# State-space scan of a hybrid decoder on one Trainium2 core: turned sample states as the moving operand in four column groups, decay products of two heads in alternation

## The chip, the cores and the metric

One core of a Trainium2 chip (TRN2) runs the whole program. The metric is the device time of one execution in microseconds, lower is better. Time before: 2363.76 us, the median of 3 runs (2363.07 to 2365.89).

## The reference, cut to what matters

The program is one inference step of a two-layer decoder trunk for a prompt of 256 tokens and 8 samples of 4 new tokens each. Layer 0 is a mixer of gated linear attention and mLSTM, layer 1 a Mamba-2 state-space mixer of 64 heads in 8 groups, with a head size of 64 and a state of 128. The change is in the scan of layer 1:

```
cb = jnp.einsum('bign,bjgn->bijg', cc, bc)
y_intra = jnp.einsum('bijgh,bjghp->bighp', cb[..., None] * decay, dtc[..., None] * xc)
y_inter = jnp.einsum('bign,bghpn->bighp', cc, s) * jnp.exp(acum)[..., None]
s_new = jnp.exp(a_last)[..., None, None] * s + jnp.einsum('bjgh,bjghp,bjgn->bghpn', w, xc, bc)
```

For a sample, `s` is the state that it brings (64 heads x 64 x 128), `cc` its C rows (4 tokens), and `y_inter` is what the old state adds to the output of the new tokens.

## The kernel before, in words

Activations lie turned, with channels on partitions and 288 columns: 256 of the prompt and 32 of the samples (sample b has columns 256 + 4b to 256 + 4b + 3). Weights are float32 and are split on the chip into a high and a low part: ScalarE casts a unit of 128x4x256 (line 126), VectorE subtracts (line 132), and TensorE makes 24 products of 288 columns with it (`project_unit`, lines 145 to 147). Four units are one quad of 256 output columns. TensorE raises the semaphore `used` at the end of a unit; ScalarE may then cast four units further on into the same buffer, and VectorE's split follows that cast.

`ssd_mixer` goes through the 8 groups of layer 1 in rounds (`turns`). A round projects group gg (5 quads, 20 units) and does the scan of the group before, G, in 20 steps between the units: step k stands behind unit k on TensorE, ScalarE and VectorE. There are eight groups, so there is a first round with projections alone, seven with both, and a last one with the scan of group 7 alone. `T_STEPS` (line 1805) is the order of TensorE's jobs, written by hand: steps 0 and 1 turn x and form C by B, step 2 turns B and the first sample's state (`st0`, line 1739), steps 2 to 9 turn the eight states and multiply them with C (`in0` to `in7`, `t_inter`, lines 1742 to 1751), steps 5, 6, 10 and 11 make the state updates (`u0` to `u7`, line 1760), steps 12 to 15 make the output of the prompt and the samples (`t_y`, lines 1773 to 1785), two heads at a time, called a quarter here, and step 18 makes the sums for the norm.

The jobs of `RING` go round three PSUM banks; those of `OWN`, `inter` among them, use a fourth. A bank is taken with a wait on the semaphore `free` and is given with `full`.

`t_inter` for sample b takes the turned state (128x512 in `stT`, two buffers by turns, written by ScalarE at line 1885) as four stationary operands of 128x128, each with the four columns of C of that sample as moving operand, all through the helper at line 1699. ScalarE may overwrite a buffer when `st_used` says so. In step 11 VectorE, behind its updates of the states (`v_update`, line 2026), multiplies the result by the exponentials of the samples (line 2079) into `inter`, and in steps 12 to 15 it adds `inter` to the output (`v_y`, line 2038).

`t_y` makes for each of two heads three products, also through line 1699: x by decay with 256 moving columns, the same with 128, and the samples' own with 32 rows and 32 columns. The first head writes partitions 0 to 63 of the bank, the second 64 to 127.

Layer 0 has helpers that matter for comparison: line 775 multiplies the samples' states with a wide query in four column groups, line 784 makes the output of a head, the last product of which sums over samples with `fold` (128x32), and line 712 makes blocks of 64 columns on two column groups.

VectorE's work for the next group (`v_prep`, lines 1942 to 1995) has the causal convolution in steps 12 to 15 and the preparation of the stacked operands in step 17. `cth` holds the tanh of the convolution between ScalarE's step 16 and VectorE's step 17. `gates1` (line 1422) makes the decay columns for the whole layer before the scan: it writes nine 64x128 blocks into `pad`, TensorE turns them, and VectorE copies them into `cols`.

Of the kernel before, what the change touches and what calls it, by code (L numbers as in the profile page):

```python
# [1411 lines left out]

K_C0, K_C1, K_CS, K_C01, K_D0, K_D1, K_DS, K_W0, K_W1, K_N = range(10)


def layer1_buffers(core, ctx):
# [3 lines left out]
def gates1(nc, core, io, scr, g):  # L1422


    with ExitStack() as tmp:
# [49 lines left out]
        @block.vector  # L1475
        def _(dve):
            st = Steps(dve, dve_s)
            dve.memset(pad[:], 0.0)
            st.then_wait(dve.tensor_copy(keep2[:], core.keep[0:64]))
            dve.memset(keep2[:, P:P + 1], 0.0)  # L1480
            dve.wait_ge(s_in, 32)
            dve.tensor_scalar(dt[:], core.bank[0][0:64, 0:T], par[:, 0:1], None, ALU.add).then_inc(u_d, 1)
            dve.wait_ge(sp_d, 1)

            st.then_wait(dve.scalar_tensor_tensor(dt[:], dt[:], 0.0, au[:], ALU.max, ALU.add))
            st.then_wait(dve.tensor_scalar(c[:], dt[:], par[:, 1:2], None, ALU.mult))
            st.then_wait(dve.tensor_tensor_scan(c[:], keep2[:], c[:], 0.0, ALU.mult, ALU.add))
            cs = samples(c[:, S0:T])
            dve.tensor_scalar(negc[:], c[:], -1.0, None, ALU.mult).then_inc(nc_d, 1)
            dve.tensor_scalar(we[:, TS:2 * TS], c[:, S0:T], -1.0, None, ALU.mult)  # L1490
            st.then_wait(dve.tensor_tensor(tot[:], c[:, P - 1:P], c[:, TP - 1:TP], ALU.add))
            dve.tensor_scalar(wx[:, 0:P], c[:, 0:P], tot[:], None, ALU.subtract)
            dve.tensor_scalar(wx[:, P:TP], c[:, P:TP], c[:, TP - 1:TP], None, ALU.subtract)
            dve.tensor_tensor(samples(wx[:, S0:T]), cs, cs[:, :, TD - 1:TD].broadcast_to([64, NB, TD]), ALU.subtract
                              ).then_inc(wx_d, 1)
            dve.tensor_copy(pad[:, 0:TP], c[:, 0:TP])
            dve.tensor_copy(pad[:, K_CS * P + 96:K_CS * P + P], c[:, S0:T])
            dve.tensor_scalar(pad[:, K_C01 * P:K_C01 * P + P], c[:, 0:P], c[:, P - 1:P], None, ALU.subtract)
            dve.tensor_copy(pad[:, K_D0 * P:K_D0 * P + TP], dt[:, 0:TP])
            dve.tensor_copy(pad[:, K_DS * P + 96:K_DS * P + P], dt[:, S0:T])  # L1500
            dve.wait_ge(wx_e, 1)
            dve.tensor_tensor(pad[:, K_W0 * P:K_W0 * P + TP], wx[:, 0:TP], dt[:, 0:TP], ALU.mult)
            dve.tensor_tensor(we[:, 0:TS], wx[:, S0:T], dt[:, S0:T], ALU.mult).then_inc(pad_d, 1)
            dve.wait_ge(turned, 1)
            for i in range(3):
                dve.tensor_copy(g["hist"][:, 16 * i:16 * i + 16].rearrange("p t c -> p (t c)"), core.bank[5 + i][:, 0:384])
            dve.wait_ge(turned, 2)
            dve.tensor_copy(g["cols"][:, 0:8].rearrange("p n h -> p (n h)"), core.bank[1][:, :])
            st.then_wait(dve.tensor_copy(g["cols"][:, 8], core.bank[2][:, 0:64]))


def ssd_mixer(nc, core, io, out, scr, g, ws):
# [6 lines left out]
    with ExitStack() as tmp:  # L1519
# [16 lines left out]
        stT, state = sb("state_turned", [P, 2, 512]), sb("state", [P, NB, 4, SSD_N])  # L1536
        y = sb("y", [P, 4, T])
        inter = sb("inter", [P, 4, TS])
        var, r, t1 = (sb(n, [P, T]) for n in ("var", "r", "t1"))
        pst = sb("prompt_state", [P, 4, P])  # L1540
        tail = sb("tail", [P, 6, 27])
# [197 lines left out]
                i = pe.transpose(bk[:, q * P:(q + 1) * P], state[:, b, q], core.ident[:])  # L1739
            i.then_inc(full_, 1)  # L1740

        def t_inter(pe, b, G):

            bk, full_ = fill("inter")
            if b == 0:
                wait_free(pe, "inter", G)
            wait_read(pe, f"st{b}", G)
            for q in range(4):
                i = mm(pe, bk[:, q * TS + TD * b:q * TS + TD * b + TD], stT[:, b % 2, q * P:(q + 1) * P],
                       xbc[:, 5, S0 + TD * b:S0 + TD * b + TD], start=True, stop=True)  # L1750
            i.then_inc(s["st_used"] if b < NB - 1 else full_, 1)

        def t_update(pe, i, G):

# [18 lines left out]
        def t_y(pe, q, G):  # L1773
            bk, full_ = fill(f"y{q}")
            wait_free(pe, f"y{q}", G)
            pe.wait_ge(s["decays"], G * 4 + (q + 1))
            if q == 0:
                pe.wait_ge(s["xsd"], G + 1)
            for hh in range(2):
                h = 2 * q + hh  # L1780
                o, c = slice(64 * hh, 64 * hh + 64), slice(64 * h, 64 * h + 64)
                mm(pe, bk[o, 0:256], xdt[:, 0, c], PP[:, h, 0:256], start=True, stop=False)
                mm(pe, bk[o, 128:256], xdt[:, 1, c], PP[:, h, 256:384], start=False, stop=True)
                i = mm(pe, bk[o, S0:T], xsr[96:128, c], PP[96:128, h, 384:416], start=True, stop=True)
            i.then_inc(full_, 1)

        def t_tail(pe, part, gg):
# [8 lines left out]
        def t_rms(pe, G):  # L1796
# [3 lines left out]
            for q in range(4):  # L1800
# [1 line left out]
            i.then_inc(full_, 1)  # L1802


        T_STEPS = {0: ("x0", "x1"), 1: ("stack", "cb"), 2: ("brow", "st0"), 3: ("st1", "in0", "st2"),
                   4: ("in1", "st3", "in2"), 5: ("u0", "u1", "in3"), 6: ("u2", "u3"), 7: ("st4", "st5"), 8: ("st6", "in4", "in5"),
                   9: ("st7", "in6"), 10: ("u4", "u5", "in7"), 11: ("u6", "u7"), 12: ("y0",), 13: ("pstate", "y1"),
                   14: ("y2",), 15: ("y3",), 18: ("rms",)}

        def t_step(pe, k, G):  # L1810
# [60 lines left out]
        def a_step(act, k, G, st):  # L1871
# [6 lines left out]
                act.activation(brow[:].rearrange("p j n -> p (j n)"), bk[:, 0:256], ACT.Copy).then_inc(s["brow"], 1)  # L1878
            for b in {2: (0,), 3: (1, 2), 4: (3,), 7: (4, 5), 8: (6,), 9: (7,)}.get(k, ()):
                bk = wait_full(act, f"st{b}", G)  # L1880
                if b >= 2:
                    act.wait_ge(s["st_used"], G * 7 + (b - 1))
                else:
                    act.wait_ge(s["tail_out"], (G + 1) * 96)
                act.activation(stT[:, b % 2], bk[:, :], ACT.Copy).then_inc(free[at(f"st{b}", 0)[0]], 1)
            if k in (5, 6):
                for q in ((0, 1), (2, 3))[k - 5]:
                    act.wait_ge(s["args"], G * 4 + (q + 1))
# [53 lines left out]
        def v_prep(dve, k, gg, st):  # L1942
# [30 lines left out]
            if k == 17:  # L1973
# [12 lines left out]
                hi = stack[:].bitcast(F32R)  # L1986
                dve.tensor_copy(hi[:, :, 0:TS], inter[:])
                dve.tensor_copy(hi[:, :, TS:2 * TS], inter[:])
                b_ = xbc[:, 4, S0:T]
                bh = bstack[:].bitcast(F32R)  # L1990
                dve.tensor_copy(bh[:, 0:TS], b_)
# [39 lines left out]
        def v_y(dve, q, G, st):  # L2031
# [3 lines left out]
            dve.scalar_tensor_tensor(y[:, q], xbc[:, q], dd[:, q:q + 1], bk[:, 0:T], ALU.mult, ALU.add  # L2035
                                     ).then_inc(free[at(f"y{q}", 0)[0]], 1)
            wait_read(dve, f"y{q}", G)
            st.then_wait(dve.tensor_tensor(y[:, q, S0:T], y[:, q, S0:T], inter[:, q], ALU.add))
            dve.tensor_tensor(y[:, q], y[:, q], zt[:, q], ALU.mult).then_inc(s["gated"], 1)

        def v_step(dve, k, G, st):
# [34 lines left out]
                dve.sem_inc(s["zg"], 1)  # L2076
            if k == 11:
                bk = wait_full(dve, "inter", G)
                dve.tensor_tensor(inter[:], bk[:, 0:4 * TS].rearrange("p (q t) -> p q t", q=4),
                                  we[:, :, TS:2 * TS], ALU.mult).then_inc(free[0], 1)  # L2080
                wait_read(dve, "inter", G)
                dve.sem_inc(s["we_used"], 1)
            if 12 <= k <= 15:
# [15 lines left out]
        def _(dve):  # L2099
            st = Steps(dve, s["dve"])  # L2100
            dve.memset(cbm[0:96, 384:416], 0.0)
            dve.memset(PP[0:96, :, 384:416], 0.0)
            st.then_wait(dve.memset(xp[:, :, 0:3], 0.0))
            dve.sem_inc(s["conv_in_used"], 1)
# [74 lines left out]
```

## Time and profile before

| | |
|---|---|
| median of 3 runs | 2363.76 us |
| the runs | 2363.07 to 2365.89 us |
| the profiled execution | 2366.03 us, its span 2364.6 us |
| mean granted clock of TensorE | 0.956 |
| TensorE busy, matmul | 2195.0 us, 93% |
| TensorE busy, weight loads | 2054.8 us, 87% |
| VectorE busy | 1438.9 us, 61% |
| ScalarE busy | 938.1 us, 40% |
| GpSimd busy | 279.1 us, 12% |
| state products of layer 1 | 66.7 us, 512 records |

How to read it: an fp32 product that is no transposition has two records in the trace, since it goes through the array in two passes; a split one (float32r) has one. Matmuls are pipelined, and their records overlap: what a product costs the queue is the distance from its start to the start of the next one, not its duration. The line of a product that was made by the helper `mm` is that of the helper, 1699, so those are told apart by their tiles and shapes. Times in the timeline are from the start of the span.

### The profile page before, as it was taken

The page shows a single profiled execution, that of the slowest core. Times are in us where ns is not written, and L with a number is a line of the kernel's source. Part 1 is how long each engine was busy: PE and PEld are TensorE (multiplying, and loading weights), DVE is VectorE, ACT ScalarE, POOL GpSimd, SP SyncE. Part 2 cuts the span into 40 slices and gives each one's busy share as a digit, 9 for nine tenths or more (in the row PEclk, how much of TensorE's full clock was granted, in tenths as well). Part 3 has the DMA queues.
Part 4 walks back from the last instruction along what each step waited for, and adds up shares of the span by engine and source line. Part 5 has one row for each costly group of instructions (what it writes and reads, how often), then busy time and mean ns, then how long its engine had stood idle before and what let it go on. Part 6 is the DMA issues. An engine that isn't in the chain of part 4 may idle for free. (4 is left out here: it accounts for less than half of the span.)

```text
span 2364.6 us, 42336 instructions
## 1 busy us (share of the span) xinstructions
PE 2195.0 (93%) x15490; PEld 2054.8 (87%) x15490; DVE 1438.9 (61%) x2784; ACT 938.1 (40%) x1260; POOL 279.1 (12%) x423
## 2 busy tenths in 40 slices
PE   6699999999999999959997899999999999859997
PEld 4698989999998998829997899989999999749996
DVE  5553756648475665744335377778778877844333
ACT  3444443444343343323333344544544435323332
POOL 1100201112001020210000102122121121210000
PEclk8799999999999999979998899999999999869999
DMA  3664858667657584747443656656565565336442
GB/s 103 215 176 127 278 157 271 195 223 239 188 172 252 151 278 121 241 168 241 153 160 120 194 144 187 181 180 189 169 189 181 159 195 179 111 136 215 158 160 75
DMA packets 332533, 427.44 MB, mean 181 GB/s; under 512 B 17133, under 2 KB 296221, under 8 KB 330977
## 3 DMA queue, kind: packets, MB, share of 16 engines
q1 hardware_dynamic: 293488, 287.16, 40.4%
q0 software_dynamic: 38720, 138.84, 16.7%
q8 instruction: 70, 1.15, 0.2%
q14 instruction: 31, 0.25, 0.0%
q10 hardware_dynamic: 224, 0.05, 0.0%
HBM read 350.63 MB, written 75.34 MB: 180 GB/s over the span
## 5 line engine op out<-in xcount | busy, mean ns | idle before, releaser
L132 DVE TENSOR_TENSOR w_lo<-w_raw,w_hi 128x1024 fp32r<-128x1024 f32 x512 | 625.1, 1224 | 676.1 <-ACT w_hi L126 668.3
L126 ACT ACTIVATE w_hi<-w_raw 128x1024 fp32r<-128x1024 f32 x512 | 540.6, 1059 | 1043.3 <-PE bank L147 981.3
L145 PE MATMUL bank<-xn_hi,w_hi 128*128 128x288 f32 x3072 | 925.6, 301 | 25.0 <-ACTq L931 12.3
L146 PE MATMUL bank<-xn_lo,w_hi 128*128 128x288 f32 x3072 | 909.4, 296 | 0.0
L147 PE MATMUL bank<-xn_hi,w_lo 128*128 128x288 f32 x3072 | 907.0, 295 | 0.0
L145 PEld LDWEIGHTS bank<-xn_hi,w_hi 128*128 128x128 f32 x3072 | 579.4, 189 | 37.5 <-issue 18.5
L146 PEld LDWEIGHTS bank<-xn_lo,w_hi 128*128 128x128 f32 x3072 | 580.4, 189 | 4.9
L147 PEld LDWEIGHTS bank<-xn_hi,w_lo 128*128 128x128 f32 x3072 | 580.9, 189 | 0.0
L145 PE MATMUL bank<-oc_o_hi,w_hi 128*128 128x288 f32 x512 | 154.5, 302 | 24.6 <-DVE oc_o_lo L1386 21.6
L145 PE MATMUL bank<-oa_o_hi,w_hi 128*128 128x288 f32 x512 | 154.3, 301 | 21.8 <-DVE oa_o_lo L1386 18.4
L146 PE MATMUL bank<-oc_o_lo,w_hi 128*128 128x288 f32 x512 | 153.8, 300 | 0.0
L147 PE MATMUL bank<-oc_o_hi,w_lo 128*128 128x288 f32 x512 | 153.5, 300 | 0.0
L146 PE MATMUL bank<-oa_o_lo,w_hi 128*128 128x288 f32 x512 | 153.5, 300 | 0.0
L147 PE MATMUL bank<-oa_o_hi,w_lo 128*128 128x288 f32 x512 | 153.2, 299 | 0.0
L145 PEld LDWEIGHTS bank<-oc_o_hi,w_hi 128*128 128x128 f32 x512 | 98.5, 192 | 25.6 <-DVE oc_o_lo L1386 22.1
L145 PEld LDWEIGHTS bank<-oa_o_hi,w_hi 128*128 128x128 f32 x512 | 98.3, 192 | 22.8 <-DVE oa_o_lo L1386 18.9
L146 PEld LDWEIGHTS bank<-oc_o_lo,w_hi 128*128 128x128 f32 x512 | 97.9, 191 | 0.3
L146 PEld LDWEIGHTS bank<-oa_o_lo,w_hi 128*128 128x128 f32 x512 | 97.7, 191 | 0.3
L147 PEld LDWEIGHTS bank<-oc_o_hi,w_lo 128*128 128x128 f32 x512 | 97.8, 191 | 0.0
L147 PEld LDWEIGHTS bank<-oa_o_hi,w_lo 128*128 128x128 f32 x512 | 97.5, 191 | 0.0
L1154 DVE SCALAR_TENSOR_TENSOR state<-state,decay,bank 128x512 f32<-128x512 f32 x128 | 90.9, 740 | 0.0
L1643 POOL DMA_DIRECT2D out_ssm_s<-ssd_state x64 | 48.0, 756 | 316.9 <-DVE ssd_state L2026 246.7
(432 smaller groups left out, 2491.5 us busy)
## 6 DMA issues: line engine op xcount, KB each, us to landing
w_raw<-in_w_in_ab SPq DMA_DIRECT2D x224, 512.0 KB, 3.8
w_raw<-in_w_in_c SPq DMA_DIRECT2D x128, 512.0 KB, 4.3
w_raw<-in_w_out_ab SPq DMA_DIRECT2D x64, 512.0 KB, 3.4
w_raw<-in_w_out_c SPq DMA_DIRECT2D x64, 512.0 KB, 3.4
state<-in_state_gla POOLq DMA_DIRECT2D x32, 512.0 KB, 10.2
out_gla_s<-state POOLq DMA_DIRECT2D x32, 512.0 KB, 4.3
state<-in_state_mlstm_c POOLq DMA_DIRECT2D x32, 512.0 KB, 9.8
out_mc_s<-state POOLq DMA_DIRECT2D x32, 512.0 KB, 4.9
```

The source lines that it names most:

```text
L126: act.activation(core.w_hi[:, j], core.w_raw[:, j % RAW], ACT.Copy).then_inc(ws["hi"], 1)
L132: dve.tensor_tensor(core.w_lo[:, j], core.w_raw[:, j % RAW], core.w_hi[:, j].bitcast(F32), ALU.subtract).then_inc(ws["split"], 1)
L145: pe.matmul(banks[m][:, 0:T], core.w_hi[:, j, kk, col], hi[:, k], start=f, stop=False)
L146: pe.matmul(banks[m][:, 0:T], core.w_hi[:, j, kk, col], lo[:, k], start=False, stop=False)
L147: ins = pe.matmul(banks[m][:, 0:T], core.w_lo[:, j, kk, col], hi[:, k], start=False, stop=e)
L1154: dve.scalar_tensor_tensor(state[:, b, kt], state[:, b, kt], dec[:, kt, b:b + 1], B[4 + i % 4][:, :], ALU.mult, ALU.add).then_inc(s["upd_d ...
L1643: pool.dma_start(ssm_out[b, bass.ds(gg * 512, 512), :].rearrange("(q p) n -> p q n", p=P), state[:, b]).then_inc(st_out[half], 16)
```

## The change

It concerns five places. The C columns of the samples go into a wide tile of zeros (`cwide`), in which sample b has 32 columns with its four at their own place. `t_inter` is called twice per group instead of eight times, once for four samples: C is the stationary operand (128x32), the turned state of a sample (128x512) the moving one, and the four samples write four column groups of one bank; the second call accumulates. It needs four buffers of turned states, of which two lie in `cth`. VectorE scales the 128x512 result in step 11 with a new column of exponentials (`K_ES`) into `irows`. In `t_y` the two heads alternate, and one more product with `fold` sums over the samples and adds to the output, for which the first quarter waits until VectorE has made `irows`. The addition in `v_y` is gone.

```diff
-K_C0, K_C1, K_CS, K_C01, K_D0, K_D1, K_DS, K_W0, K_W1, K_N = range(10)
+K_C0, K_C1, K_CS, K_C01, K_D0, K_D1, K_DS, K_W0, K_W1, K_ES, K_N = range(11)
...
+            dve.tensor_copy(pad[:, K_ES * P:K_ES * P + P].rearrange("p (g t) -> p g t", g=4),
+                            we[:, TS:2 * TS].unsqueeze(1).broadcast_to([64, 4, TS]))
...
-            st.then_wait(dve.tensor_copy(g["cols"][:, 8], core.bank[2][:, 0:64]))
+            st.then_wait(dve.tensor_copy(g["cols"][:, 8:10].rearrange("p n h -> p (n h)"), core.bank[2][:, 0:128]))
...
+        cwide = sb("c_wide", [P, T])
+        spare = cth[:].rearrange("p m c -> p (m c)")
+        turned = [stT[:, 0], stT[:, 1], spare[:, 0:512], spare[:, 512:1024]]
+        irows = spare[:, 1024:1536]
...
-        def t_inter(pe, b, G):
+        def t_inter(pe, half, G):
             bk, full_ = fill("inter")
-            if b == 0:
+            if half == 0:
                 wait_free(pe, "inter", G)
-            wait_read(pe, f"st{b}", G)
-            for q in range(4):
-                i = mm(pe, bk[:, q * TS + TD * b:q * TS + TD * b + TD], stT[:, b % 2, q * P:(q + 1) * P],
-                       xbc[:, 5, S0 + TD * b:S0 + TD * b + TD], start=True, stop=True)
-            i.then_inc(s["st_used"] if b < NB - 1 else full_, 1)
+            wait_read(pe, f"st{4 * half + 3}", G)
+            for g_ in range(4):
+                i = pe.matmul(bk[TS * g_:TS * g_ + TS, :], cwide[:, TS * (4 * half + g_):TS * (4 * half + g_) + TS], turned[g_], start=half == 0, stop=half == 1)
+            i.then_inc(full_ if half else s["st_used"], 1)
...
             if q == 0:
                 pe.wait_ge(s["xsd"], G + 1)
-            for hh in range(2):
-                h = 2 * q + hh
-                o, c = slice(64 * hh, 64 * hh + 64), slice(64 * h, 64 * h + 64)
+                wait_read(pe, "inter", G)
+            halves = [(slice(64 * hh, 64 * hh + 64), 2 * q + hh, slice(128 * q + 64 * hh, 128 * q + 64 * hh + 64)) for hh in range(2)]
+            for o, h, c in halves:
                 mm(pe, bk[o, 0:256], xdt[:, 0, c], PP[:, h, 0:256], start=True, stop=False)
+            for o, h, c in halves:
                 mm(pe, bk[o, 128:256], xdt[:, 1, c], PP[:, h, 256:384], start=False, stop=True)
-                i = mm(pe, bk[o, S0:T], xsr[96:128, c], PP[96:128, h, 384:416], start=True, stop=True)
+            for o, h, c in halves:
+                mm(pe, bk[o, S0:T], xsr[96:128, c], PP[96:128, h, 384:416], start=True, stop=False)
+            i = mm(pe, bk[:, S0:T], irows[:, q * P:(q + 1) * P], core.fold[:], start=False, stop=True)
             i.then_inc(full_, 1)
...
-        T_STEPS = {0: ("x0", "x1"), 1: ("stack", "cb"), 2: ("brow", "st0"), 3: ("st1", "in0", "st2"),
-                   4: ("in1", "st3", "in2"), 5: ("u0", "u1", "in3"), 6: ("u2", "u3"), 7: ("st4", "st5"), 8: ("st6", "in4", "in5"),
-                   9: ("st7", "in6"), 10: ("u4", "u5", "in7"), 11: ("u6", "u7"), 12: ("y0",), 13: ("pstate", "y1"),
+        T_STEPS = {0: ("x0", "x1"), 1: ("stack", "cb"), 2: ("brow", "st0"), 3: ("st1", "st2"),
+                   4: ("st3",), 5: ("u0", "u1", "in0"), 6: ("u2", "u3"), 7: ("st4", "st5"), 8: ("st6",),
+                   9: ("st7",), 10: ("u4", "u5", "in1"), 11: ("u6", "u7"), 12: ("y0",), 13: ("pstate", "y1"),
...
-                if b >= 2:
-                    act.wait_ge(s["st_used"], G * 7 + (b - 1))
-                else:
+                if b >= 4:
+                    act.wait_ge(s["st_used"], G + 1)
+                elif b < 2:
                     act.wait_ge(s["tail_out"], (G + 1) * 96)
-                act.activation(stT[:, b % 2], bk[:, :], ACT.Copy).then_inc(free[at(f"st{b}", 0)[0]], 1)
+                act.activation(turned[b % 4], bk[:, :], ACT.Copy).then_inc(free[at(f"st{b}", 0)[0]], 1)
...
+                dve.tensor_copy(samples(cwide[:], TS + TD)[:, :, 0:TD], samples(xbc[:, 5, S0:T]))
...
-            st.then_wait(dve.tensor_tensor(y[:, q, S0:T], y[:, q, S0:T], inter[:, q], ALU.add))
...
-                dve.tensor_tensor(inter[:], bk[:, 0:4 * TS].rearrange("p (q t) -> p q t", q=4),
-                                  we[:, :, TS:2 * TS], ALU.mult).then_inc(free[0], 1)
+                dve.tensor_tensor(irows.rearrange("p (h c) -> p h c", c=64), bk[:].rearrange("p (h c) -> p h c", c=64),
+                                  cc[:, K_ES].unsqueeze(2).broadcast_to([P, 8, 64]), ALU.mult).then_inc(free[0], 1)
...
+            dve.memset(cwide[:], 0.0)
```

## Rows read from the trace of the kernel before

**Rows 1.** The page: engine busy time, and the granted clock in 40 slices.

```profile
PE 2195.0 (93%) x15490; PEld 2054.8 (87%) x15490; DVE 1438.9 (61%) x2784; ACT 938.1 (40%) x1260; POOL 279.1 (12%) x423
...
PEclk8799999999999999979998899999999999869999
```

**Rows 2.** Busy time by stretch: PE, PEld, DVE, ACT, POOL, clock, DMA share, GB/s.

```profile
1580.00:1670.00 90.00, 88.60 (x655) 83.63 (x653) 73.36 (x180) 38.68 (x60) 18.10 (x27) 1.00 0.58 174
```

**Rows 3.** Waits of TensorE, 1490 to 2030: us in total, times, longest.

```profile
PE bank L145 <- ACT ssd_z L1868: 4.8, 5, 1.0
```

**Rows 4.** Timeline, TensorE, first projection product of two rounds: start us, us.

```profile
1575.16 0.39 PE L145 MATMUL bank<-xn_hi,w_hi 128*128 128x288 f32 x1 [0.96 <-ACT ssd_z L1868]
...
1669.24 0.39 PE L145 MATMUL bank<-xn_hi,w_hi 128*128 128x288 f32 x1 [0.96 <-ACT ssd_z L1868]
```

**Rows 5.** Timeline, TensorE, step 9: a state block and what follows.

```profile
1619.26 0.95 PE L1699 MATMUL bank<-ssd_xbc,ssd_state_turned 128*128 128x4 f32 x8
1620.07 0.38 PE L145 MATMUL bank<-xn_hi,w_hi 128*128 128x288 f32 x1
```

**Rows 6.** Timeline, TensorE, step 3: a state block and the next transposition.

```profile
1590.70 0.95 PE L1699 MATMUL bank<-ssd_xbc,ssd_state_turned 128*128 128x4 f32 x8
1592.09 0.66 PE L1739 MATMUL bank<-ident,ssd_state 128*128 128x128 f32 x4 [0.44 <-DVE ssd_b3m L2062]
```

**Rows 7.** Timeline, TensorE, layer 0: sample states in four column groups.

```profile
497.68 3.64 PE L775 MATMUL bank<-state,proj 128*32 128x512 f32 x32
501.25 0.40 PE L145 MATMUL bank<-xn_hi,w_hi 128*128 128x288 f32 x1
```

**Rows 8.** Timeline, TensorE, step 12: a quarter of the decay products.

```profile
1631.65 0.86 PE L1699 MATMUL bank<-ssd_decay,ssd_x_dt_rows 128*64 128x256 f32 x4
1632.44 0.30 PE L1699 MATMUL bank<-ssd_decay,ssd_x_sample_rows 32*64 32x32 f32 x2
...
1633.69 0.40 PE L145 MATMUL bank<-xn_hi,w_hi 128*128 128x288 f32 x1
```

**Rows 9.** Timeline, TensorE, layer 0: blocks of 64 columns on two column groups.

```profile
178.62 0.73 PE L712 MATMUL bank<-factors,k_factor 128*64 128x64 f32 x16
```

**Rows 10.** Timeline, TensorE, layer 0: the product with fold and what follows.

```profile
516.63 0.41 PE L784 MATMUL bank<-fold,proj 128*128 128x32 f32 x2
516.87 0.90 PE L784 MATMUL bank<-att,v_rows 128*128 128x256 f32 x4
```

**Rows 11.** Timeline, ScalarE and VectorE, steps 11 and 12: cast, split, updates, scaling.

```profile
1628.10 1.06 ACT L126 ACTIVATE w_hi<-w_raw 128x1024 fp32r<-128x1024 f32 x1 [3.49 <-PE bank L147]
...
1629.19 1.23 DVE L132 TENSOR_TENSOR w_lo<-w_raw,w_hi 128x1024 fp32r<-128x1024 f32 x1 [1.02 <-ACT w_hi L126]
1630.33 2.38 DVE L2026 SCALAR_TENSOR_TENSOR ssd_state<-ssd_state,ssd_we,bank 128x128 f32<-128x128 f32 x8
1632.93 0.29 DVE L2079 TENSOR_TENSOR ssd_inter<-bank,ssd_we 128x128 f32<-128x128 f32 x1 [0.22 <-DVE ssd_state L2026]
```

**Rows 12.** Timeline, VectorE, step 0: x rows by a column.

```profile
1677.35 0.69 DVE L2002 TENSOR_TENSOR ssd_x_dt_rows<-bank,ssd_cols_cur 128x512 f32<-128x512 f32 x1
```

**Rows 13.** Two gaps of TensorE (timeline), and the clock after the first (by stretch).

```profile
858.33 0.40 PE L145 MATMUL bank<-xn_hi,w_hi 128*128 128x288 f32 x1 [1.98 <-ACT proj L869]
...
727.70 0.40 PE L145 MATMUL bank<-xn_hi,w_hi 128*128 128x288 f32 x1 [2.21 <-DVE w_lo L132]
...
859.20:862.50 3.30, 3.30 (x16) 3.30 (x15) 0.13 (x1) 0.00 (x0) 2.58 (x4) 0.50 0.84 254
862.60:866.00 3.40, 3.40 (x28) 3.40 (x27) 1.23 (x1) 1.06 (x1) 3.40 (x6) 1.00 0.84 235
```

**Rows 14.** Timeline, last group: VectorE's updates and scaling, TensorE's first quarter.

```profile
2078.69 2.39 DVE L2026 SCALAR_TENSOR_TENSOR ssd_state<-ssd_state,ssd_we,bank 128x128 f32<-128x128 f32 x8 [2.32 <-PE bank L1760]
...
2083.79 0.29 DVE L2079 TENSOR_TENSOR ssd_inter<-bank,ssd_we 128x128 f32<-128x128 f32 x1
...
2081.57 1.54 PE L1699 MATMUL bank<-ssd_decay,ssd_x_dt_rows 128*64 128x256 f32 x4
```

## The prediction

> **What bounds the kernel now.** I began with the page. TensorE is busy for 93% of the span and its clock is granted in full almost everywhere [rows 1]. The change sits in the state-space scan of layer 1, so I then took busy times by stretch: in the steady part TensorE works 88.60 of 90 us at clock 1.00, VectorE 73.36 and ScalarE 38.68 [rows 2]. In the list of waits, the longest one that TensorE had in 540 us of that part comes to 4.8 us in total [rows 3]. The first projection product of two successive rounds starts at 1575.16 and 1669.24, so one round (20 projection units of one group, with the scan of the group before in between) takes 94.08 us [rows 4]. TensorE paces the scan, and a saving on its queue counts in full, seven times, except where it already waits. The timeline shows where that is, and where it will wait in future.
>
> **The change, part by part, for one of the seven steady rounds.**
>
> *State products, removed.* A sample's block is four fp32 products, eight records, with 128 columns of weights and four moving columns; it occupies the queue from 1619.26 to 1620.07, 0.81 us [rows 5]. There are eight in a round. The block in step 3 saves nothing: after it TensorE still idled 0.44 us for VectorE's read of the B rows, which ends at the same time with or without it, so the second transposition stays at 1592.09 [rows 6]. Seven blocks count: 5.67 us.
>
> *State products, added.* Two blocks of four products, 32 weight columns and 512 moving columns each, every product in its own column group. Layer 0 does just this with 16 products: 32 records of 592 ns or more in 3.57 us from first start to the next projection [rows 7]. So the four groups run at once, 0.43 us for each set of four records, with some 0.13 us for entering and leaving. Eight records are two sets: 0.86 + 0.2 = 1.06 us a block, 2.12 us in all. Net: 5.67 - 2.12 = 3.55 us saved.
>
> The fourfold overlap is what the row shows: 32 records one after another, at the 0.43 us that each needs, would be 13.8 us. The Trainium skill, "TensorE: Matmul & The Clock Gate", Part 3 (packing small matmuls), gives a speedup of 2.38 for three column tiles with 512 columns. By an estimate from that ratio (79% of perfect) the two blocks would cost about 0.5 us more and the total gain would be some 3 us smaller. The trace has the same operation at nearly perfect overlap, so the row decides.
>
> *Decay products.* A quarter (two heads) now takes 1631.65 to 1633.69, 2.04 us: 0.79 for the 256- and 128-column products of a head up to its 32-row product at 1632.44, then 0.23 for that, and the other head the same [rows 8]. The two heads write different halves of the array's columns. Today the first head's 32-row product, another shape on the same columns, stands between them and they run in series. With the heads alternating, the wide products of both should overlap. The nearest row is layer 0's 64-column block: 16 records, fp32, two column groups, in 0.73 us of which the last record alone is 222 ns; that is 34 ns per record, where a record of one group takes 53 ns or more (0.23 us for two records with their change of shape) [rows 8, 9]. So 0.79 us holds both heads' wide products, about 0.25 both heads' 32-row products with the change of shape. The added product with the fold matrix is 128 by 128 with 32 moving columns; layer 0 has it at 0.24 us (516.63 to 516.87) [rows 10]. Sum 1.28, I take 1.30 us. Bounds: no overlap gives 2.04 + 0.24 - 0.1 = 2.2 us, perfect overlap of everything 1.2. Saved: 0.74 x 4 = 2.96 us.
>
> *The new wait in front of the first decay product.* That product now waits until VectorE has read the state products and scaled them. This work stands in VectorE's queue behind the updates of step 11, and those behind a weight split which waits for ScalarE, which waits for projection unit 11: cast at 1628.10, split at 1629.19, updates 1630.33 to 1632.71, and the read at 1632.93 [rows 11]. The read grows from 128x128 (0.29 us) to 128x512 out of PSUM times a broadcast column, the form of the row at 0.69 us [rows 12]. It ends at 1633.62, TensorE sees it near 1633.67, and its first decay product would be ready at 1631.65 [rows 8]. **A stall of 2.02 us per round that was not there.** It does not shrink when TensorE gets faster, since its start hangs on TensorE's own unit 11. Bounds: 1.7 (the read at 0.4 us) and 2.4. Queued behind it on TensorE are the rest of the quarters and unit 13; their splits are more than 10 us early. On VectorE the next split and first quarter come 0.4 us later, which its idle time takes.
>
> *What the stall does to the clock.* Gaps of this size exist before. After 1.98 us the stretch 859.20 to 862.50 ran at clock 0.50, with 16 records where the next 3.4 us held 28; after 2.21 us at 727.70 nothing fell [rows 13]. A fall costs (28 - 16)/28 x 3.4 = 1.45 us. I take four falls in seven rounds, 5.8 us; ends 0 and 7 x 1.45 = 10.2.
>
> *Costed at nothing in the steady rounds:* VectorE's copy of C into the wide tile and its longer read, less four small adds and their self-waits, lie in its idle time (90 - 73.36 us per 90 [rows 2]); without that cover they would cost about 0.3 us a round. ScalarE's copies of turned states now wait once for a half instead of seven times for a block; with four buffers they never wait. No transfer moves.
>
> *Sum of a steady round:* -3.55 - 2.96 + 2.02 = -4.49 us. Seven rounds: -31.4; the first has no earlier group's norm before it, so step 3 gains there too: -0.6.
>
> *Last group, without projections.* It runs at half clock and VectorE paces much of it. VectorE idled 2.32 us before the updates of samples 4 to 7 for TensorE, because of the state products; that goes. But the first decay product started at 2081.57, before the read at 2083.79, and must now follow it: 2083.79 - 2.32 + 0.73 = 2082.2 [rows 14]. Then the shorter quarters give back 2 to 3 us if the clock comes up as it did, and lose about as much if TensorE, with less work before, stays at half clock. I take -1 us, ends -4 and +3.
>
> *Preparing the layer.* One more transposition and one more VectorE write of 64x128 before the scan, the write below the 0.29 us of a 128x128 one [rows 11]: +0.4 us, ends 0 and 1.
>
> **Sum:** -32.0 - 1.0 + 0.4 + 5.8 = -26.8 us. The profiled execution took 2366.03 us (span 2364.6), 2.3 us above the median of the runs; from it the result is 2339.2, against the median 2363.76 it is **2337 us**.
>
> **The rivals.** (A) *The two heads do not overlap*, so the alternation does not do what it says. For it: no row has 64 columns by 256 moving. Against it: the 64-column block in layer 0 [rows 9]. A quarter would then be 2.2 us, a loss of 0.16 x 4 instead of a gain of 2.96: 3.6 x 7 = 25 us more, 2362 us.
>
> (B) *VectorE takes over steps 4 to 9.* It is without idle time from the norm of the previous group to about step 6, and step 3 is already its own. If it also holds back the blocks taken out of steps 4 and 5 and bank releases of step 6, 1.6 us more per round are lost: 11 us, 2348 us. Against it: the weight splits there are 8 to 11 us early.
>
> (C) *Slower: the clock does not come back after the stall.* Place: from the first decay product on. Price: 1.45 us for each 3.4 us at half clock. The change turns into a loss once there are more than (31 + 2)/1.45 = 22 such stretches, over three a round. If all of step 12 to 19, some 33 us, ran at half clock, each round would lose 14 us: 2363.76 - 32.6 + 98 = 2429 us. For it: TensorE stood at half clock in the last group. Against it: the gap of 1.98 us cost one stretch and no more [rows 13].
>
> **How the numbers follow.** Forecast 0.76, A 0.07, B 0.13, C 0.03, the rest for something unforeseen that gains more. The forecast's own bounds: no fall of the clock and a good last group give 2328, seven falls, a longer stall (0.4 x 7) and a bad last group 2348, where B lies as well. Range 2327 to 2349. What a measurement of this kernel can tell from no change is about 0.2%, 4.7 us. Only A and part of the unforeseen fall within it: same 0.05; slower 0.04; faster 0.91.
>
> **What would show it.** In the new profile: state products of 128x32 by 512, eight records twice a round, two sets of four starts 0.43 us apart; a quarter of 1.3 us with records of both heads starting within some 15 ns; a wait of TensorE on VectorE's scaling of about 2.0 us in each steady round, the first decay product's; rounds of about 89.6 us, plus 1.5 where the clock falls; no new waits for splits. The prediction is wrong if the stall is absent or above 3 us, if quarters stay near 2 us, or if step 3's second transposition moves.

## The result and the profile after

The changed kernel takes 2332.16 us, the median of four runs (2327.44 to 2340.6), against 2363.57 of four runs of the kernel before (2363.07 to 2365.89): a ratio of 0.9865, with a 95% interval of 0.9851 to 0.9879, 31.4 us less. The forecast was 2337, with a range of 2327 to 2349. The profiled execution took 2328.8 us, its span 2327.3. In the experiments one execution, of the kernel with the wide products in series, took 3046.71 us at a mean granted clock of 0.644; it counts in that kernel's median and not in its ratio, and nothing is read from it.

The page of the changed kernel has engine busy time and the granted clock in 40 slices, against [rows 1]:

```profile
span 2327.3 us, 41668 instructions
...
PE 2131.6 (92%) x15171; PEld 1983.0 (85%) x15171; DVE 1436.1 (62%) x2762; ACT 937.9 (40%) x1260; POOL 279.8 (12%) x423
...
PEclk8799999999999999978999799999999999869999
```

TensorE has 63 us less work, and the span is only 37 us shorter. The other 26 us are new idle time of TensorE: seven waits of 1.96 us in front of a first quarter (13.7), 0.8 us more in step 3 of six rounds (4.8), and most of the rest in the last group, where it waits 4.2 us in front of the first quarter. One round shows the first two. Its timeline has the first projection product of two rounds, and between them a block of state products (step 5) and the first quarter (step 12), against [rows 4, 5, 8]:

```profile
1562.51 0.40 PE L145 MATMUL bank<-xn_hi,w_hi 128*128 128x288 f32 x1 [0.96 <-ACT ssd_z L1876]
...
1579.46 0.65 PE L1745 MATMUL bank<-ident,ssd_state 128*128 128x128 f32 x4 [1.24 <-DVE ssd_b3m L2070]
...
1587.32 0.62 PE L1755 MATMUL bank<-ssd_state_turned,ssd_c_wide 128*32 128x512 f32 x2
1587.34 0.62 PE L1755 MATMUL bank<-ssd_conv_tanh,ssd_c_wide 128*32 128x512 f32 x2
1587.78 0.60 PE L1755 MATMUL bank<-ssd_state_turned,ssd_c_wide 128*32 128x512 f32 x2
1587.79 0.60 PE L1755 MATMUL bank<-ssd_conv_tanh,ssd_c_wide 128*32 128x512 f32 x2
1588.32 0.40 PE L145 MATMUL bank<-xn_hi,w_hi 128*128 128x288 f32 x1
...
1617.22 0.87 PE L1705 MATMUL bank<-ssd_decay,ssd_x_dt_rows 128*64 128x256 f32 x8 [1.96 <-DVE ssd_conv_tanh L2087]
1618.02 0.30 PE L1705 MATMUL bank<-ssd_decay,ssd_x_sample_rows 32*64 32x32 f32 x4
1618.26 0.41 PE L1705 MATMUL bank<-fold,ssd_conv_tanh 128*128 128x32 f32 x2
1618.50 0.38 PE L145 MATMUL bank<-xn_hi,w_hi 128*128 128x288 f32 x1
...
1651.67 0.40 PE L145 MATMUL bank<-xn_hi,w_hi 128*128 128x288 f32 x1 [0.96 <-ACT ssd_z L1876]
```

One round is 89.16 us, where it was 94.08. The state products start four at a time, two sets 0.45 us apart, and the block takes 1.00 us. A quarter takes 1.28 us instead of 2.04, with the 256-column products of both heads 7 ns apart (1617.222 and 1617.229). In front of the first quarter TensorE stands for 1.96 us. Also, the second transposition of step 3 now waits 1.24 us for VectorE's B rows instead of 0.44 [rows 6]: the block taken out there has turned into idle time, as the prediction had it. The transposition itself starts 16.95 us after the first product of the round, where it was 16.93.

TensorE's waits in the changed kernel, 1480 to 2000 (us in total, times, longest), against [rows 3]:

```profile
PE bank L1705 <- DVE ssd_conv_tanh L2087: 11.8, 6, 2.0
PE bank L1745 <- DVE ssd_b3m L2070: 7.5, 6, 1.3
PE bank L145 <- ACT ssd_z L1876: 4.8, 5, 1.0
```

The first line is the change's own wait, on the scaling. VectorE's timeline has the queue in which that stands, against [rows 11]:

```profile
1612.73 1.23 DVE L132 TENSOR_TENSOR w_lo<-w_raw,w_hi 128x1024 fp32r<-128x1024 f32 x1 [1.29 <-ACT w_hi L126]
1613.87 2.39 DVE L2035 SCALAR_TENSOR_TENSOR ssd_state<-ssd_state,ssd_we,bank 128x128 f32<-128x128 f32 x8
1616.48 0.69 DVE L2087 TENSOR_TENSOR ssd_conv_tanh<-bank,ssd_cols_cur 128x512 f32<-128x512 f32 x1 [0.22 <-DVE ssd_state L2035]
```

**Round by round**, from unit 19 to the next unit 19. Before: 93.33, then six of 94.08 to 94.10. After: 87.58, 90.67, 89.16, 89.17, 89.17, 90.70, 92.19. The three that stand out from 89.17, the second and the last two, are those in which the granted clock fell to half around the end of the wait. Here is the first, in the timeline of TensorE and by stretch (us, then busy time of PE, PEld, DVE, ACT and POOL, clock, DMA share, GB/s):

```profile
1526.56 0.87 PE L1705 MATMUL bank<-ssd_decay,ssd_x_dt_rows 128*64 128x256 f32 x8 [1.96 <-DVE ssd_conv_tanh L2087]
```

```profile
1524.90:1528.20 3.30, 1.65 (x17) 1.29 (x18) 2.77 (x6) 0.79 (x1) 1.84 (x3) 1.00 0.59 212
1528.30:1531.60 3.30, 3.30 (x16) 3.30 (x15) 3.19 (x10) 0.00 (x0) 1.05 (x2) 0.50 0.82 197
1531.70:1535.00 3.30, 3.30 (x30) 3.04 (x31) 1.09 (x1) 1.38 (x2) 0.06 (x1) 1.00 0.49 189
```

**Step by step** (start of a unit to the start of the next, in one round without a fall, before and after). Step 4: 5.36 and 3.63. Step 5: 4.55 and 4.82. Step 8: 5.41 and 3.62. Step 9: 4.53 and 3.63. Step 10: 4.55 and 4.82. Step 12: 5.33 and 6.60. Steps 13 to 15: 7.22 and 6.42, 5.86 and 5.08, 5.43 and 4.64. The other steps differ by no more than a few hundredths. So the state products give 3.88 us (steps 4, 5, 8, 9 and 10), the quarters 3 x 0.79 (steps 13 to 15), and step 12 costs 1.27, which is 2.06 for the wait less 0.79 for its quarter.

The seven rounds sum to 657.88 and 628.64 us, 29.2 less. From the last product of the last unit to the first one of the output projection it is 76.87 and 74.94, 1.9 less. The two profiled spans differ by 37.3 us because parts that the change doesn't touch differ as well: some 3.5 us before the scan, where the profile of before has two stretches at half clock at 992 to 1006 that the other lacks, and 2.6 behind it. The medians, 31.4 apart, are the measure.

### The profile page after: what moved, and what is told of

Its sections match the earlier page's. It is cut to its first block and busy times, and to the rows that moved or that the text cites. A ratio compares the mean times of both kernels' runs of the same rounds, so it can differ in the third digit from the quotient of the medians.

```text
span 2327.3 us, 41668 instructions
## 1 busy us (share of the span) xinstructions
PE 2131.6 (92%) x15171; PEld 1983.0 (85%) x15171; DVE 1436.1 (62%) x2762; ACT 937.9 (40%) x1260; POOL 279.8 (12%) x423
```

## The experiments

The kernel before was measured again beside them, and each ratio is against the time measured beside it: 2365.8 us for the first four, 2364.37 for the last four.

### The state products alone

The changed kernel, with one head's three products ahead of the other's again:

```diff
             for o, h, c in halves:
                 mm(pe, bk[o, 0:256], xdt[:, 0, c], PP[:, h, 0:256], start=True, stop=False)
-            for o, h, c in halves:
                 mm(pe, bk[o, 128:256], xdt[:, 1, c], PP[:, h, 256:384], start=False, stop=True)
-            for o, h, c in halves:
                 mm(pe, bk[o, S0:T], xsr[96:128, c], PP[96:128, h, 384:416], start=True, stop=False)
```

> The changed kernel, but the two heads of a quarter in series again, each with its 32-row product behind its wide ones, then the fold product. Theory (a product of another shape between the heads keeps them apart): a quarter takes the 2.04 us of before plus the fold product's 0.24, about 2.27 us against 1.28 in the changed kernel, so a steady round is 4.0 us longer and the time 28 us above the changed kernel's 2332, near 2360. Rival (the array overlaps the heads in any order, the alternation does nothing): quarters stay at 1.3 us and the time at 2332.

Measured: 2373.82 us against 2365.8, ratio 1.0034 (1.0019 to 1.005). Half of the change, alone, makes the kernel slower, by 8 us. The theory on the quarters holds (a round without a fall is 4.0 us above the 89.17 of the changed kernel), but its time of 2360 was missed by 14 us: 6 of them are more time at half clock than in the changed kernel, 4 lie in the last group, and 2 in the time of the kernel before, which was that much longer on this occasion. Its rounds: 91.61, 96.19, 96.25, 96.22, 93.21, 93.19, 96.23. Where the clock holds, a round is 93.2 and beats the 94.09 of before by 0.9; in four of the seven it falls, and each fall costs 3.0 us. The rounds sum to 662.9 us, 5.0 more than before, and the last group (79.17 us up to the output projection against 76.87) adds 2.3. The timeline of one and its stretches:

```profile
1630.70 0.86 PE L1705 MATMUL bank<-ssd_decay,ssd_x_dt_rows 128*64 128x256 f32 x4 [1.96 <-DVE ssd_conv_tanh L2085]
1631.50 0.30 PE L1705 MATMUL bank<-ssd_decay,ssd_x_sample_rows 32*64 32x32 f32 x2
1631.72 1.51 PE L1705 MATMUL bank<-ssd_decay,ssd_x_dt_rows 128*64 128x256 f32 x4
```

```profile
1626.50:1631.70 5.20, 3.24 (x23) 2.66 (x22) 4.60 (x11) 1.46 (x4) 1.20 (x2) 1.00 0.48 144
1631.80:1638.60 6.80, 6.80 (x27) 6.01 (x28) 3.62 (x11) 0.00 (x0) 1.69 (x3) 0.50 0.71 231
1638.60:1642.00 3.40, 3.40 (x28) 2.95 (x26) 1.22 (x1) 1.65 (x2) 3.08 (x5) 1.00 0.45 118
```

The gap is the same 1.96 us. What differs from the changed kernel is that the products right behind it run one head after the other, on half of the array's columns, and the half clock lasts 6.8 us in all four falls, where there two of three last 3.4. That the one causes the other is not shown, and there is a rival: in the kernels with both halves at work (the changed one, and those with the wide products in series and with the scaling one split later) the half clock lasts 3.4 us in all seven falls that start 1.6 to 1.9 us after the gap's end, and 6.8 in all five that start at most 0.6 us after it or before it. Of the four falls here one starts 0.4 us after it, where theirs last 6.8 us too, and two 1.1 us after it, where they have none, so that only the fourth (1.70 us after it, against 3.4 us of half clock at 1.71 in the changed kernel) speaks for the narrow products.

### The alternation alone

The kernel before, with nothing changed but the order of the two heads:

```diff
-            for hh in range(2):
...
+            for o, h, c in halves:
                 mm(pe, bk[o, 0:256], xdt[:, 0, c], PP[:, h, 0:256], start=True, stop=False)
+            for o, h, c in halves:
                 mm(pe, bk[o, 128:256], xdt[:, 1, c], PP[:, h, 256:384], start=False, stop=True)
+            for o, h, c in halves:
                 i = mm(pe, bk[o, S0:T], xsr[96:128, c], PP[96:128, h, 384:416], start=True, stop=True)
```

> The kernel before with the alternation of the two heads alone: no wide C, no fold product, no new wait. Theory: a quarter falls from 2.04 to about 1.02 us, a steady round from 94.1 to 90.0, and the time by 29 us for seven rounds and 2 to 4 in the last group, to about 2332: as much as the whole change gives, since the state products' gain of 3.9 us a round is used up by the fold product (1.0) and the new wait (2.1). Rival (the state products are what pays, as in the prediction's terms of 3.55 against 2.96 before the wait): the alternation alone gives 21 us or less, 2343 or more.

Measured: 2335.35 us (2332.68 to 2339.71), ratio 0.9873 (0.9857 to 0.989), 30.4 us less than the kernel before. A reordering of six products has nearly the whole gain of the change. A quarter in its timeline is 1.04 us, there is no new wait, and the six later rounds are 90.07 to 90.09, which is 4.0 = 4 x 1.0 less than before:

```profile
1712.08 0.87 PE L1699 MATMUL bank<-ssd_decay,ssd_x_dt_rows 128*64 128x256 f32 x8
1712.88 0.30 PE L1699 MATMUL bank<-ssd_decay,ssd_x_sample_rows 32*64 32x32 f32 x4
1713.12 0.40 PE L145 MATMUL bank<-xn_hi,w_hi 128*128 128x288 f32 x1
```

### The wide products of a head in series

The changed kernel, with the 256- and the 128-column product of the first head, then those of the second, and both 32-row products behind:

```diff
                 mm(pe, bk[o, 0:256], xdt[:, 0, c], PP[:, h, 0:256], start=True, stop=False)
-            for o, h, c in halves:
                 mm(pe, bk[o, 128:256], xdt[:, 1, c], PP[:, h, 256:384], start=False, stop=True)
```

> The changed kernel, but within a quarter both wide products of the first head, then both of the second, then the two 32-row products, then fold: no alternation, and nothing of another shape between the heads. Theory (each column group takes its own products as they come, some ahead of the others, as the first four of the state products start within 20 ns although each has a second pass first in order): the second head starts within 20 ns of the first, the quarter stays at 1.28 us, the time at 2332. Rival (products start strictly in order, so that only neighbours in the order overlap): the second head waits until the first one's last wide product starts, 0.5 us later, a quarter takes about 1.8 us, a round 2.1 us more, the time about 2347.

Measured: 2332.0 us (three of the four runs 2327.74 to 2334.3), ratio 0.985 (0.983 to 0.9871), the same as the changed kernel. The two heads' first records start 13 ns apart (1709.896 and 1709.909), and the quarter looks as it did:

```profile
1709.90 0.88 PE L1705 MATMUL bank<-ssd_decay,ssd_x_dt_rows 128*64 128x256 f32 x8 [1.96 <-DVE ssd_conv_tanh L2086]
1710.70 0.30 PE L1705 MATMUL bank<-ssd_decay,ssd_x_sample_rows 32*64 32x32 f32 x4
```

So it isn't alternation that makes them overlap. All four records with 256 columns start (1709.896 to 1710.176) before any with 128 (1710.378 on), although the first head's 128-column product stands ahead of the second head's 256-column one in the program. What kept the heads apart before was the 32-row product between them. Program order is that of kernel.py here; no run shows the compiled stream. The Trainium skill, "TensorE: Matmul & The Clock Gate", Part 3 (The mechanism), says that products start and end in program order, with no reordering; these records, on two halves of the columns, do not start so, and the measurement decides. The Trainium skill, "TensorEngine Tiling (Array Packing)", Key Properties, says that TensorE drains when the shape of its tiles changes; with that the first experiment, in which the second head starts only behind the first one's 32-row product (1631.50, 1631.72), agrees. It doesn't single out the shape, though: a third product of the same shape on the same columns in that place might hold the second head back too, and that wasn't tried.

### The scaling ahead of the updates

The changed kernel, with VectorE's scaling of the state products moved ahead of the two state updates in its queue, within step 11:

```diff
+            if k == 11:
+                bk = wait_full(dve, "inter", G)
+                dve.tensor_tensor(irows.rearrange("p (h c) -> p h c", c=64), bk[:].rearrange("p (h c) -> p h c", c=64),
+                                  cc[:, K_ES].unsqueeze(2).broadcast_to([P, 8, 64]), ALU.mult).then_inc(free[0], 1)
+                wait_read(dve, "inter", G)
+                dve.sem_inc(s["we_used"], 1)
             for i in {5: (0, 1), 6: (2, 3), 10: (4, 5), 11: (6, 7)}.get(k, ()):
                 v_update(dve, i, G, st)
...
-            if k == 11:
...
```

> The changed kernel with one edit on VectorE: in step 11 the scaling of the state products stands ahead of the last two updates of states instead of behind them. Theory: the scaling then ends about 2.6 us earlier, before the first decay product is ready, so the wait of 1.96 us goes, a steady round falls from 89.2 to about 87.1 us, no stretch at half clock is left in the steady rounds, and the time falls to about 2314 with runs within 0.3% of each other. Rival (the wait only moves: the updates now come 0.9 us later and TensorE waits for their bank, or for the decay factors): a wait of 1 us or more stands in step 12 or 13 and the time is 2325 or above. Second rival, on the clock: falls come without the gap too, and the runs still differ by 10 us.

Measured: 2310.88 us (2308.63 to 2312.93), ratio 0.9768 (0.9752 to 0.9784): 54.9 us less than before, where the change has 31.4. The four runs lie 4.3 us apart, those of the changed kernel 13.2. The rounds are 85.54 and then 87.11 to 87.15, no clock falls in them, and the wait is gone from TensorE's list (1480 to 1970):

```profile
PE bank L1745 <- DVE ssd_b3m L2070: 7.4, 6, 1.2
PE bank L145 <- ACT ssd_z L1876: 4.8, 5, 1.0
```

VectorE's timeline in the same place, with the two groups changed round, and TensorE's first decay product, which starts without a wait while VectorE is still at the updates:

```profile
1694.99 1.23 DVE L132 TENSOR_TENSOR w_lo<-w_raw,w_hi 128x1024 fp32r<-128x1024 f32 x1 [1.30 <-ACT w_hi L126]
1696.13 0.68 DVE L2079 TENSOR_TENSOR ssd_conv_tanh<-bank,ssd_cols_cur 128x512 f32<-128x512 f32 x1
1697.04 2.39 DVE L2035 SCALAR_TENSOR_TENSOR ssd_state<-ssd_state,ssd_we,bank 128x128 f32<-128x128 f32 x8 [0.23 <-DVE ssd_conv_tanh L2079]
...
1697.45 0.87 PE L1705 MATMUL bank<-ssd_decay,ssd_x_dt_rows 128*64 128x256 f32 x8
```

The medians of the two kernels are 21.3 us apart, their profiled spans 20.3. In the seven rounds it is 20.3 us: 7 x 2.04 = 14.3 for the wait and 6.0 for the falls. The last group gives 2.2 more (its wait is 1.64 us where it was 4.18), which parts that the edit doesn't touch take back in these two profiles.

### The state products alone, with the scaling ahead

The first and the fourth edit together.

> The states part alone (heads in series as in the kernel before) with the scaling ahead of the last updates, so without the new wait. Theory: a steady round is 91.2 us against 94.1 before and 93.2 with the wait, and no stretch at half clock is left; seven rounds give 20 us, the time is about 2343. So the states part was slower than the kernel before only through the wait and the clock. Rival (the narrow products by themselves bring the clock down, without a gap): stretches at half clock remain in half of the rounds and the time is 2353 or more.

Measured: 2344.71 us, ratio 0.9907 (0.988 to 0.9933). Rounds 89.57 and 91.15 to 91.18, none with a fall: 2.9 less than before. The state products are worth that much, which is their 3.88 less 4 x 0.24 for the products with fold. In the first experiment the wait (2.04 a round) and the falls (12 us in four rounds) had taken more than that.

### The wait at the product that needs it

The changed kernel, with the wait moved from the first decay product to the first product with fold:

```diff
-                wait_read(pe, "inter", G)
...
+            if q == 0:
+                wait_read(pe, "inter", G)
             i = mm(pe, bk[:, S0:T], irows[:, q * P:(q + 1) * P], core.fold[:], start=False, stop=True)
```

> The changed kernel with TensorE's wait for the scaled state products moved from the front of the first quarter to its last product, the only one that reads them. Theory: the first quarter's other products fill 0.9 us of the gap, so the wait falls from 1.96 to about 1.1 us, a steady round from 89.2 to 88.3, and fewer stretches at half clock follow: time 2320 to 2326. Rival (gap length is not what brings the clock down): as many falls as before, 2326 and the same spread of 10 us between runs.

Measured: 2321.37 us (2320.92 to 2324.02), ratio 0.9816 (0.9792 to 0.9841). The gap is 0.93 us, the six later rounds are 88.11 to 88.14, and no clock falls in them, where the theory had fewer falls. What the gap has in front of it is different too, the first quarter's other products instead of a projection unit:

```profile
1704.21 0.30 PE L1705 MATMUL bank<-ssd_decay,ssd_x_sample_rows 32*64 32x32 f32 x4
1705.43 0.41 PE L1705 MATMUL bank<-fold,ssd_conv_tanh 128*128 128x32 f32 x2 [0.93 <-DVE ssd_conv_tanh L2088]
```

### The scaling one split later

The changed kernel, with the scaling in VectorE's step 12, behind one more weight split:

```diff
-            if k == 11:
+            if k == 12:
```

> The changed kernel with the scaling moved from step 11 to step 12 on VectorE, behind one more weight split, so that TensorE's wait grows from 1.96 to about 3.1 us. Theory: a steady round without a fall of the clock is 90.3 us; the longer gap brings the clock down in every round, for one or two stretches of 3.4 us (1.5 us each), so that rounds measure 91.8 to 93.3 and the time 2348 to 2360. Rival (falls of the clock are chance and not tied to the gap): two or three of seven rounds fall as in the changed kernel, and the time is 2340.

Measured: 2350.24 us (2345.17 to 2351.89), ratio 0.9931 (0.9903 to 0.9958). The gap is 3.12 us, and the clock falls in all seven rounds, in four of them for 6.8 us and in three for 3.4; the first four rounds are 91.73, 93.09, 91.83 and 92.81 us. Without a fall it would be about 90.3, an estimate from the 87.13 of the fourth experiment and the wait. One of them, in the timeline and by stretch:

```profile
1628.16 0.87 PE L1705 MATMUL bank<-ssd_decay,ssd_x_dt_rows 128*64 128x256 f32 x8 [3.12 <-DVE ssd_conv_tanh L2087]
```

```profile
1630.00:1633.30 3.30, 3.30 (x16) 3.30 (x15) 2.96 (x10) 0.00 (x0) 0.00 (x0) 0.51 1.00 356
```

### A fuller step 0

The fourth experiment's kernel, with three moves in TensorE's order, to see whether VectorE is next in line: a transposition out of step 3, where TensorE waits, into 4; two jobs of step 1 into step 0, where it waits for ScalarE; and an update from step 6 into 7:

```diff
-        T_STEPS = {0: ("x0", "x1"), 1: ("stack", "cb"), 2: ("brow", "st0"), 3: ("st1", "st2"),
-                   4: ("st3",), 5: ("u0", "u1", "in0"), 6: ("u2", "u3"), 7: ("st4", "st5"), 8: ("st6",),
+        T_STEPS = {0: ("x0", "x1", "stack", "cb"), 2: ("brow", "st0"), 3: ("st1",),
+                   4: ("st2", "st3"), 5: ("u0", "u1", "in0"), 6: ("u2",), 7: ("u3", "st4", "st5"), 8: ("st6",),
```

ScalarE's copy of the third state (`st2`) and VectorE's fourth update (`u3`) follow into steps 4 and 7.

> The changed kernel with the scaling first, and three more edits of order: the third state's transposition in step 4 instead of 3 (TensorE waits 1.24 us there), the stack and the C by B products in step 0 where TensorE waits 0.96 us for ScalarE, and the fourth update in step 7 on both engines. Theory A (those waits are free time on TensorE): a round falls by 2.2 us from 87.1 to 84.9 and the time by 15 from 2311 to about 2296. Theory B (VectorE, without idle time from the norm to step 6, is next in line there, as rival B of the prediction had it): most of it comes back as waits for updates or banks in steps 5 to 8, the round stays above 86.3 and the time above 2305.

Measured: 2306.35 us (2305.27 to 2309.99), ratio 0.9755 (0.9729 to 0.978), the fastest median of all, though its interval overlaps with that of the fourth experiment (0.9752 to 0.9784). Its six later rounds are 86.91 to 86.92, 0.2 less than the fourth experiment's. Both waits that were attacked are gone from the list, and others stand there (1480 to 1970):

```profile
PE bank L1745 <- DVEq L2038: 10.4, 6, 1.7
PE bank L1745 <- DVE ssd_x_w_rows L2011: 1.7, 6, 0.3
```

The sum of the list is 12.1 us where it was 12.2. The bank that VectorE gives back with its update of step 6 (`u2`, done at about 1590) now comes 1.7 us late for the transposition of `st5`, and VectorE is busy for 27.94 of the 30 us from 1561 to 1591: with the change's gain taken, VectorE paces steps 0 to 7.

## Why the prediction was right

None of the signs of being wrong that the prediction set came: the stall is 1.96 us, a quarter 1.28, and step 3's second transposition stays where it was in the round.

**State products removed.** Predicted 0.81 us a block; measured 0.88, from the five that left steps 4, 8 and 9 (1.73 + 1.79 + 0.90 = 4.42). The distance in [rows 5], from the block's start to the next projection product, is thus 0.07 us too small for what a block costs its step; where those hundredths lie was not looked at.

**State products added.** Predicted 1.06 us; from the block's start to the next projection product it is 1.00, at nearly perfect overlap, as layer 0's row had it and the ratio of 2.38, which the prediction has from the Trainium skill, had not. By the steps, as for the removed ones, a block costs 0.88 + 0.27 = 1.15 us, since steps 5 and 10 lost one old block, gained one new and became 0.27 longer. Together 4.42 - 2 x 0.27 = 3.88 us instead of 3.55.

**Quarters.** Predicted 1.30 us, measured 1.28. That the heads would overlap was right, and so was the reason given, that the 32-row product kept them apart: the first and third experiments are a pair that shows it. That it did so by its shape, and not as one more product on the same columns, is not shown. The row used for the sum, layer 0's 64-column block, has the records of one column half some 58 ns apart (178.784, 178.843 and 178.901), so the 53 ns of the prediction is only a lower bound. Rival A (2362 us) has fallen.

**The wait.** Predicted 2.02 us, measured 1.96 (4.18 in the last group), from the chain of the prediction: split, updates, scaling. The fourth experiment takes away only what stood ahead of it, and 2.04 us a round come back. In the last group the first decay product was to start 38.7 us behind the last product of the last unit; it starts 38.9 behind it.

**The clock.** Predicted four falls of 1.45 us in seven rounds. Measured, in the profiled run, four stretches of 3.4 us, two of them joined, in three rounds: 1.5 + 1.5 + 3.0 = 6.0 us. That this hit so closely owes something to luck: in the two kernels with the same gap, the first and third experiment, it was four and two rounds of seven, at 3.0 and 1.5 us. The four runs of the changed kernel lie 13 us apart, and the slower ones have the lower mean granted clock: 0.956 at 2327.44 us, 0.955 at 2328.8, 0.953 at 2335.52 and 0.952 at 2340.6. That suggests that the median has more time at half clock than the profiled run; how much, and whether it lies in the scan, is not known.

**The steady round and the sum.** Predicted -4.49, measured -4.93 without a fall (in the first round -5.1 and -5.75); over seven rounds 3 us, which is most of the distance from 2337 to 2332. The last group with its surroundings gave 1.9 us (its own part up to the store of oT 1.6) against 1, and the preparation of the gates cost 0.2 us against 0.4.

**Rival B**, VectorE in steps 4 to 9, was not in this change: the removed blocks of steps 4, 8 and 9 came back in full. It is next, though, as the last experiment shows. **Rival C**, the clock that does not come back, was wrong for 1.96 us, where every fall ended after 3.4 or 6.8 us. But falls of the clock are what makes half of the change, alone, slower than nothing (four of 3.0 us; without them it would be some 4 us faster), and the experiments show them growing with the gap: in seven rounds no fall at 0 and 0.93 us, two to four at 1.96, seven at 3.12. All 16 of those falls start between 1.2 us before and 1.9 us after the end of such a gap.

What the prediction didn't see is how the gain is made up. The state products, the larger part of the edit, pay 3.88 us a round, and the product with fold (1.0), the wait (2.0) and the clock (0.9 in the mean of the profiled run) take all of it back. The alternation alone pays the 4.0. The prediction priced each of these terms but never summed them part by part, or it would have seen that the part with the wait stood at nothing (by its own terms 3.55 against 0.96 for fold, 2.02 for the wait and 0.83 for the clock), with its price in one place of VectorE's queue.

Not tried: a product of the same shape in the place of the 32-row one between the heads, a gap between 0.93 and 1.96 us, the same gap with wide and with narrow products behind it and nothing else changed, and VectorE's steps 0 to 7 in a shorter form.

## What to carry to other kernels

Keep a product of another tile shape out from between products that write different column groups: with two products for each group their order among themselves did not matter, and the one odd product between them cost 1 us in 2. When a result gets a new reader, look at what stands ahead of it in the producer's queue: moving one instruction ahead of two updates brought the gain from 31 to 55 us. And sum a change by parts, each with the wait it brings and what that does to the clock, since one part may be paying for the other.

## What was not expected of the hardware

Products of two column halves start out of the order of the program: in the third experiment the second head's 256-column product starts 13 ns after the first head's (1709.896 and 1709.909), before the first head's 128-column one (1710.378).

A gap of 1.96 us brings a fall of the granted clock to 0.50 in some rounds only: three, two and four of seven in three kernels with the same gap. Its length differs too, 3.4 us in four of the five falls where both halves of the array work behind the gap, 6.8 in all four where one does, and 6.8 in four of seven behind a gap of 3.12 us. Where both halves work, it goes by when the fall starts: 3.4 us in the seven that start 1.6 us or more behind the gap's end, 6.8 in the five that start earlier. At 0.93 us there was no fall.
